# Gate and up products as seven block products of half width, their weight sums on GpSimd

## What is computed

```python
def rms_norm(x, g):
    y = xf * lax.rsqrt(jnp.mean(xf * xf, axis=-1, keepdims=True) + EPS)
    return (y * g.astype(jnp.float32)).astype(x.dtype)

def swiglu_ffn(h, w_gate, w_up, w_down):
    return (jax.nn.silu(h @ w_gate) * (h @ w_up)) @ w_down
...
        x = x + y                                   # y: the mixer's output
        h = rms_norm(x, norm_ffn_g[i])
        x = x + swiglu_ffn(h, ffn_w_gate[i], ffn_w_up[i], ffn_w_down[i])
    return rms_norm(x, final_norm_g)
```

## Time and profile before

| | us |
|---|---|
| median of 3 runs | 1129.02 (1127.19 to 1129.13) |
| the profiled execution | 1129.12 |
| its span in the profile | 1127.2 |
| PE busy | 1107.1 (98%) |
| DVE busy | 606.3 (54%) |
| ACT busy | 392.5 (35%) |
| POOL busy | 100.9 (9%) |

### The profile page before, as it was taken

How to read it: one execution, slowest core, us unless ns; L and a number is a source line. 1 busy time by engine, 2 the same in 40 slices (tenths; PEclk the granted TensorE clock), 3 DMA queues, 4 the chain that set the end, 5 groups by cost and what they waited for, 6 DMA issues and landing times.

```text
span 1127.2 us, 14278 instructions
## 1 busy us (share of the span) xinstructions
PE 1107.1 (98%) x5046; PEld 902.8 (80%) x5046; DVE 606.3 (54%) x867; ACT 392.5 (35%) x582; POOL 100.9 (9%) x91
## 2 busy tenths in 40 slices
PE   8999999999999999999999988999999999999997
PEld 7888888888888888888877755778888888888887
DVE  5855567644444443334577899485454444433333
ACT  6222233433333422222345466244333333222222
POOL 6000025000000000111200000150000000001110
PEclk9999999999999999999999999999999999999999
DMA  7333433333333322333332011033333333223321
GB/s 197 105 93 93 128 96 105 102 94 93 93 110 93 94 65 77 103 103 108 99 94 73 3 35 41 19 113 111 95 93 93 104 93 101 65 77 103 91 75 75
DMA packets 189793, 101.61 MB, mean 90 GB/s; under 512 B 4616, under 2 KB 188096, under 8 KB 189760
## 3 DMA queue, kind: packets, MB, share of 16 engines
q1 hardware_dynamic: 189408, 100.61, 30.5%
q0 software_dynamic: 320, 0.55, 0.2%
q10 hardware_dynamic: 32, 0.01, 0.0%
HBM read 99.06 MB, written 2.10 MB: 90 GB/s over the span
## 4 chain that ended last, share of the span: by engine, by line
PE 85%; DVE 10%; ACT 3%; issue 1%; POOL 0%; DVEq 0%; POOLq 0%; ACTq 0%
PE ps L360 27%; PE ps L361 27%; PE ps L362 27%; DVE wgt_lo L344 3%; DVE prob L976 1%; ACT prob L683 1%; PE ps L1229 1%; DVE prob L992 1%; DVE xg_lo L763 1%; DVE inv_lat L433 1%; ACT xg_hi L541 0%; DVE xT L825 0%; PE ps L1290 0%; PE ps L1306 0%; PE ps L1106 0%
## 5 line engine op out<-in xcount | busy, mean ns | idle before, releaser
L360 PE MATMUL ps<-xg_hi,wgt_hi 128*128 128x512 f32 x936 | 366.8, 392 | 0.2 <-DVE c_r L790 0.2
L362 PE MATMUL ps<-xg_hi,wgt_lo 128*128 128x512 f32 x936 | 364.2, 389 | 0.0
L361 PE MATMUL ps<-xg_lo,wgt_hi 128*128 128x512 f32 x936 | 364.2, 389 | 0.0
L344 DVE TENSOR_TENSOR wgt_lo<-raw,wgt_hi 128x1024 fp32r<-128x1024 f32 (+3 forms) x219 | 263.2, 1208 | 183.6 <-ACT wgt_hi L335 182.7
L335 ACT ACTIVATE wgt_hi<-raw 128x1024 fp32r<-128x1024 f32 (+3 forms) x219 | 199.4, 919 | 294.1 <-PE ps L362 291.2
L360 PE MATMUL ps<-hid_hi,wgt_hi 128*128 128x512 f32 (+1 forms) x550 | 211.6, 385 | 0.0
L362 PE MATMUL ps<-hid_hi,wgt_lo 128*128 128x512 f32 (+1 forms) x550 | 209.5, 381 | 0.0
L361 PE MATMUL ps<-hid_lo,wgt_hi 128*128 128x512 f32 (+1 forms) x550 | 209.5, 381 | 0.0
L360 PEld LDWEIGHTS ps<-xg_hi,wgt_hi 128*128 128x128 f32 x936 | 175.7, 188 | 38.5 <-issue 1.8
L361 PEld LDWEIGHTS ps<-xg_lo,wgt_hi 128*128 128x128 f32 x936 | 175.7, 188 | 37.5 <-issue 1.2
L362 PEld LDWEIGHTS ps<-xg_hi,wgt_lo 128*128 128x128 f32 x936 | 175.7, 188 | 36.4
(11 more groups left out here) (127 smaller groups left out, 632.1 us busy)
## 6 DMA issues: line engine op xcount, KB each, us to landing
raw<-in_ffn_w_gate SPq DMA_DIRECT2D x44, 512.0 KB, 3.8
raw<-in_ffn_w_up SPq DMA_DIRECT2D x44, 512.0 KB, 3.9
raw<-in_conv_w_in SPq DMA_DIRECT2D x24, 512.0 KB, 3.8
raw<-in_ffn_w_down SPq DMA_DIRECT2D x32, 384.0 KB, 3.1
raw<-in_ffn_w_down SPq DMA_DIRECT2D x32, 320.0 KB, 2.9
raw<-in_conv_w_out SPq DMA_DIRECT2D x8, 512.0 KB, 3.7
raw<-in_mla_w_o SPq DMA_DIRECT2D x8, 512.0 KB, 3.8
x_nat<-in_x SPq DMA_DIRECT2D x4, 512.0 KB, 6.8
```

The costliest lines, as they stand in the source:

```text
L344: ins = nc.vector.tensor_tensor(dst, src, hi.bitcast(F32), ALU.subtract)
L360: nc.tensor.matmul(acc, wh, xh, start=first, stop=False)
L361: nc.tensor.matmul(acc, wh, xl, start=False, stop=False)
L362: return nc.tensor.matmul(acc, wl, xh, start=False, stop=last)
```

## The change

The gate product of one body (and likewise the up product) is a matrix of 2 hidden chunks by 512 tokens with 8 feature chunks summed over. It is taken as a 2 by 2 by 2 block product: two hidden chunks, two token halves of 256, even and odd feature chunks. Instead of eight block products it makes seven, from sums of blocks (Winograd's form of Strassen's scheme). Each of the seven is 4 chunks by 3 matmuls of 256 columns: 84 matmuls of 256 columns where there were 48 of 512.

- Weights: a group is the gate or the up slab of a chunk pair, 128x8x256, one load of 1 MB into `pair_raw` (two buffers, which overlay `raw`). Four of its seven operands are sums of blocks; POOL makes them into `w_sum` (`weight_sums`), each 128x512. ACT splits off the high part of all seven (`make_op_hi`), DVE the rest (`make_op_lo`), 128x512 each, one group ahead of PE.
- Tokens: `out_body` makes seven operands per pair of x chunks, `x_op_hi` and `x_op_lo`: ACT writes the gained halves to `stage`, DVE makes one difference after an even chunk and three after an odd one, ACT and DVE split them.
- Results: ACT copies the first product (`s1`), DVE makes the four blocks by five additions from PSUM in a group of up (four in a group of gate), scales gate by `inv`, ACT applies Silu to 128x1024, DVE multiplies the pair.
- `inv` of the up part moves to the down product: `scaled_residual` is two DVE instructions where `residual` is one.
- The high and low parts of the hidden layer are made during the groups for chunks 0 to 9 and after the last group for the other twelve. The memory map moves to make this fit.

```diff
+            def load_group(l, i, par):
...
+                    wait_apart(sp, op_lo, op_no(l, i, par, 0) - OPS)
+                m = (gates, ups)[par][l]
+                sp.dma_start(pair_raw[:, par, :, :], m[:, :, ds(i * (2 * P), 2 * P)]).then_inc(pair_in[par], 16)
...
+            def weight_sums(l, i, par):
...
+                nc.gpsimd.tensor_tensor(wide(w_sum, 0), b["A21"], b["A22"], ALU.add).then_inc(sum_done, 1)
...
+                    wait(pool, op_lo, free + 3)
+                wait(pool, sum_done, done + 1)
+                nc.gpsimd.tensor_tensor(wide(w_sum, 1), wide(w_sum, 0), b["A11"], ALU.subtract).then_inc(sum_done, 1)
...
+                nc.gpsimd.tensor_tensor(wide(w_sum, 2), b["A11"], b["A21"], ALU.subtract).then_inc(sum_done, 1)
...
+                nc.gpsimd.tensor_tensor(wide(w_sum, 3), b["A12"], wide(w_sum, 1), ALU.subtract).then_inc(sum_done, 1)
...
+                    with pool.Fori(0, DC // 2) as m:
+                        add_square(n, m, tile_free, m + (T0[name] + 1))
+                    weight_sums(n // 2, 0, 0)
+                    with pool.Fori(DC // 2, DC) as m:
+                        add_square(n, m, tile_free, m + (T0[name] + 1))
...
+            def scaled_residual(l, m, bank, used):
+
+                wait(ve, w_used, used)
+                nc.vector.tensor_tensor(res[:, :], ps[:, bank, :], inv[:, :], ALU.mult).then_inc(res_new, 1)
+                wait(ve, res_new, m + (DC * l + 1))
+                nc.vector.tensor_tensor(chunk(xT, m), res[:, :], chunk(xT, m), ALU.add).then_inc(tile_free, 1)
...
+                    residual(m, u, U0[name] + m + 1)
+                    ve.wait_ge(xg_new, DC * l + m + 1)
+                    if m % 2 == 0:
+                        nc.vector.tensor_tensor(stage[:, 2, :], stage[:, 0, :], stage[:, 1, :],
+                                                ALU.subtract).then_inc(t_new, 1)
+                        weights()
+                        x_op_lo_of(l, c, 0, 0, 2)
...
+                    for p in range(4):
+                        weights(p)
+                    wait(ve, op_used, op0 + 5)
+                    wait(ve, s1_done, g + 1)
...
+                        nc.vector.tensor_tensor(pair[:, 3, :], halves[:, 0, :], s1[:, :], ALU.add)
+                        nc.vector.tensor_tensor(u2, halves[:, 1, :], s1[:, :], ALU.add).then_inc(u2_done, 1)
...
+                    weights(4)
+                    wait(ve, u2_done, g + 1)
+                    nc.vector.tensor_tensor(w_u3[:, :, :], ps[:, b0 + 2, :].rearrange("p (h n) -> p h n", h=2),
+                                            u2.unsqueeze(1).broadcast_to([P, 2, N]), ALU.add).then_inc(w_u3_done, 1)
+                    weights(5)
...
+                    wait(ve, op_used, op0 + 7)
...
+                    weights(6)
...
+            def seven_product(l, i, par, p, ks, first=False):
...
+                    if first:
+                        pe.wait_ge(x_op_done, 12 * l + 3 * k + (1, 1, 2, 2, 3, 3, 3)[p])
+                    col = slice(k * P, (k + 1) * P)
+                    ins = product(acc, op_w_hi[:, p, col], op_w_lo[:, p, col],
+                                  x_op_hi[:, k, x, :], x_op_lo[:, k, x, :], k == 0, k == DC // 2 - 1)
...
+                seven_product(l, 0, 0, 2, quarters[:3], True)
+                seven_product(l, 0, 0, 3, quarters[:3], True)
+                seven_product(l, 0, 0, 2, quarters[3:], True)
+                seven_product(l, 0, 0, 3, quarters[3:], True)
+                statistic(norm)
```

More of the change, by code:

```diff
@@ L473, in _ @@
                             load_unit(sp, name, i, u)
+                if name in ("conv_out", "mla_out"):
+                    l = int(name == "mla_out")
+                    for par in range(2):
+                        load_group(l, 0, par)
+                    with sp.Fori(1, PAIRS_F) as i:
+                        for par in range(2):
+                            load_group(l, i, par)
             for t in range(TB):
@@ new lines, in out_body @@
+            def out_body(name, i):
+                l = int(name == "mla_out")
+                for u in range(4):
+                    m = 4 * i + u
+                    c = m // 2
+                    sc.wait_ge(tile_free, T0[name] + m + 1)
+                    if m > 1:
+                        wait(sc, x_op_done, 12 * l + 3 * c)
+                    at = (0, 5)[m % 2]
+                    nc.scalar.activation(stage[:, at:at + 2, :], xT[:, m, :].rearrange("p (a s) -> p a s", a=2), ACT.Copy,
+                                         scale=gain[:, rows[f"ffn{l}"] + m:rows[f"ffn{l}"] + m + 1]).then_inc(xg_new, 1)
+                    if m % 2 == 0:
+                        x_op_hi_of(l, c, 0, 0, 2)
+                    else:
+                        x_op_hi_of(l, c, 1, 2, 4)
+                        x_op_hi_of(l, c, 2, 4, 7)
+                    if i == 0:
+                        unit_hi(sc, name, 1, u)
+                    else:
+                        sc.wait_ge(w_used, U0[name] + 4 + u + 1)
+                        for p in range(2 * u, min(2 * u + 2, OPS)):
+                            make_op_hi(sc, l, 0, 0, p)
```

368 lines of the change are left out of this document (276 added, 92 removed).

## The result

The changed kernel takes 1154.31 us (median of 4 runs, 1153.24 to 1155.1), the kernel before 1128.96 (4 runs, 1127.19 to 1129.13). The ratio is 1.0226, with a 95% interval of 1.0214 to 1.0239: 2.3% slower, 25.3 us. The forecast was slower by 50 us; the measured time lies in its range, not at its centre.

The account below looks back on a forecast made before the run. PE bounded gate and up; after the change DVE, stretched by POOL's sums, would. Layers +21.5 and +24.2 us, clock +3.4, end +0.5: together +49.6 on 1129.1, predicting 1179 us, range 1125 to 1215.

Parts of the forecast that it names:

- The bound, and its change: Gate and up: PE bounds it before; afterwards DVE, stretched by POOL, needs 21.8 or 23.0 us a body against PE's 20.2.
- DVE's own work: Gate and up bodies: DVE's instructions without stalls take 15.2 us, or 16.4 in the five bodies that also write hidden rests.
- The stall: Gate and up bodies: of eight POOL sums two fall free and six cost DVE 1.1 us each, 6.6 us a body.
- The hand-over: Entry to gate and up: first gate group ends 60.4 us after the first residual; PE, ready at 33.1 or 28.3, waits.
- The clock: Hand-overs: after each of two long PE waits the lower clock costs half of 3.4 us, +3.4 in all.
- The load: Weight loads of 1 MB in gate and up: 6.2 us each, upper bound twice 6.8, covered by the buffer loop.
- D: Rival, gate and up: 1 MB loads come late, at 13.6 us, bodies some 23.9 us; 1209 us, chance 0.08.
- The down product: After gate and up: unchanged, as ten of 22 hidden chunks are ready and give 6.8 us of cover.
- B: Rival, gate and up: sums cost DVE nothing in effect below 0.6 us of stall each, bodies 20.2; 1115 us, chance 0.14.
- C: Rival, gate and up: a POOL sum over strided blocks takes 1.6 us, bodies 1.8 us longer; 1219 us, chance 0.12.
- E: Rival: a stall is 0.7 us instead of 1.1, bodies 20.6 and 20.2, each hand-over 4 us shorter; 1131 us, chance 0.06.
- F: Rival, gate and up: narrow matmuls come no closer than 0.130 us, 21.8 a body on PE; 1179 us, chance 0.05.

Follow-up runs that it names:

- Run 1: The changed kernel with each POOL weight sum replaced by an 8-element addition and a fill, so the sums are left out: 1119.34 us.
- Run 3: The changed kernel with the third weight sum of each group computed twice on POOL: 1194.01 us.
- run 7: The changed kernel with all weight sums on DVE, placed late (three of a group's four behind weight rest 5, one behind rest 6): 1156.3 us.
- run 4: The changed kernel with the sums of each layer's first gate and first up group replaced by fills: 1143.67 us.
- run 8: The changed kernel with 26 spare matmuls of 128 columns ahead of the last quarter of the first gate product: 1158.65 us.
- run 9: The changed kernel with the weight sums left out and 26 spare matmuls ahead of the first gate product's last quarter: 1117.99 us.
- Run 2: The changed kernel with all weight sums on DVE, placed early (three of a group's four behind weight rests 0 to 3, one behind rest 5): 1229.48 us.
- runs 5 and 10: The changed kernel with hidden low parts of two tile pairs instead of five written inside gate and up: 1149.55 us; the same with weight sums left out: 1123.21 us.
- run 6: The changed kernel with hidden low parts of four tile pairs instead of five written inside gate and up: 1153.97 us.

## Why the prediction was right, and where it was off

**The bound, and its change: right.** PE held the stage at 100% before, and the matmuls of 256 columns come at 0.120: 20.16 a body where PE sets the pace. DVE sets it otherwise, through a stall that only instructions with two SBUF inputs suffer. Run 1 takes the sums' reads away, and with them some of POOL's time, and with them goes all of the loss; DVE's busy time falls by 46 us a layer with the same instructions. Run 3 adds two sums and the bodies grow.

**DVE's own work: 0.6 too low late, 1.2 too low early.** I had 15.2 and 16.4; run 7 gives 15.8 and 17.6, with waits for ACT of about 0.4 in a late body and 1.0 in an early one. The records of the two rows of rests agree with the earlier trace rows.

**The stall: the term that was mis-sized.** The step "six cost 1.1: 6.6 us" gave too much. No sum was free, as I had assumed of two, but only three instructions a body lost the full 1.1; the others were hit for part of a sum, with a PSUM instruction beside the rest. By the records it is 5.4 us a body, 0.67 a sum; at the body's pace 4.5, 0.56 a sum, because the waits for ACT shrink by some of it. The Trainium skill, "SBUF — State Buffer", section "Who interferes with whom", has the later instruction blocked for the whole of the earlier one. The 2.31 rows bear that out where a sum falls on one instruction only; for the 1.30 of every sum it is too much here, and it would have put the forecast 24 us further off. The sum's own length I had right: 1.30 at 307.17, with blocks of 128 elements too. The estimate of 1.12 from the Trainium skill, "GPSIMD Engine Reference", section 3.1, is 0.18 below this row.

In bodies 1 to 5 the error is 23.0 - 22.2 = 0.8, 3.8 us a layer. In bodies 6 to 10 it is more, 21.8 - 20.5: with 4.5 of stall DVE needs 15.8 + 4.5 = 20.3, which is PE's 20.16 to within 0.1, and it took two bodies until DVE had caught up. My point from which the sums would cost nothing, 0.6 a sum, is 0.55 with the work that run 7 shows, (20.16 - 15.8) / 8, and the measured 0.56 lies on it. So the late bodies stand at the balance of the two engines, which is luck, and the early ones, with 17.6 of own work, do not. The two errors make 10 us a layer, 20 of the 25 by which the forecast was too high.

**The hand-over: right, in its sum and in DVE's row.** Forecast 60.4 us from the first residual to the end of the first gate group, measured 60.1 and 60.1. Chunk 6's x rest let PE go on after 47.4 and 47.3 us, forecast 47.4, and the last x rests were written after 56.1 and 56.0, forecast 56; PE's three products follow. The row of the latter in layer 0:

```profile
208.98 3.75 DVE L1010 TENSOR_TENSOR x_op_lo<-stage,x_op_hi 128x512 fp32r<-128x512 f32 x2
```

The sums' share was nearly right: I had 3.7 and 3.3 us; without them (run 4) PE goes on after 43.7 and the last x rests are there after 49.6, 3.7 and then 2.7 us less. The group itself ends only 5.2 and 4.7 us earlier there, as PE, still behind from its low clock, is then the last. Wrong was when PE comes ready: not after 33.1 and 28.3 us but after 36.9 and 37.5. In layer 1 mla_out's last products wait for a rest that stands behind the stalled x rests. DVE's two rows, and PE's first matmul behind its wait:

```profile
757.09 3.70 DVE L1010 TENSOR_TENSOR x_op_lo<-stage,x_op_hi 128x512 fp32r<-128x512 f32 x2
760.71 2.28 DVE L359 TENSOR_TENSOR wgt_lo<-raw,wgt_hi 128x1024 fp32r<-128x1024 f32 x1
...
763.14 0.77 PE L375 MATMUL ps<-hid_hi,wgt_hi 128*128 128x512 f32 x1 [5.36 <-DVE wgt_lo L359]
```

Since DVE's row sets the end, it didn't matter when PE arrived.

**The clock: 3.4 us counted that were not on the path.** I added them to a sum whose end DVE sets. The lower clock did come (0.74 in the window where the products run), but behind it PE waits 0.72 and 0.67 us more for DVE, so the matmuls' delay is hidden (run 8). Once the sums don't stall DVE this second wait is gone and the clock does count (run 9).

**The load: 5.2 us, not 6.2**, by the median of issue to landing; POOL waits for it, 2.23 us in the body shown. I had named such waits as a sign that I was wrong (D); they are there, 111 us in all, and nothing comes of them, for run 1 has them too beside bodies of 20.16. Run 2 shows what such a wait costs on DVE.

**The down product: its cover is real.** I counted ten ready chunks as cover and left them alone. With four, PE pays 1.6 to 2.5 us a layer (runs 5 and 10); with eight nothing in layer 0, and at most 0.7 us in layer 1 (run 6). The half-microsecond at the end was right.

**The rivals.** B (the sums cost nothing in effect) holds for the last bodies alone; had it held everywhere, run 1 is what it looks like, 1119 against my 1115. C falls: sums that needn't wait take 1.30, and only with DVE beside them up to 2.3. D falls with the load at 5.2. E had the size of the stall about right (six at 0.7 are 4.2 us, measured 4.5), but the early bodies too short (20.6, for DVE's own work was 1.2 more) and the hand-overs wrong (4 us shorter each). F falls with 0.120.

**The signs.** PE is idle for 7% of gate and up, not 10%. Its waits for x rests come to 19.3 us in both layers together, where I had 14 and 19. The weight rests beside a sum do not form one kind near 1.8: they run from 0.85 to 1.8, as a sum mostly hits them in part.

## What to carry to other kernels

Work that is moved to an idle engine is not free when both engines read SBUF: here eight sums of 1.30 us on POOL cost DVE 4.5 us a body, while computing them on DVE itself cost 4.9. Before trading matmul time for additions, add up DVE's instructions with two SBUF inputs and charge each addition on POOL four to eight tenths of its length; if that passes the matmuls' time, the trade loses in that stage. Charge a lower clock only where its engine does not wait again behind the slow stretch, and give an engine that has other work no wait for a load in the middle of its row.
